# Transposing x with a diagonal of inverse roots at two layer ends of a transformer trunk, instead of scaling it first

## The reference

```python
def rmsnorm(x, g):
    y = xf * lax.rsqrt(jnp.mean(xf * xf, axis=-1, keepdims=True) + EPS)
    return (y * g.astype(jnp.float32)).astype(x.dtype)

def modulate(h, shift, scale):
    return h * (1 + scale[:, None, :]) + shift[:, None, :]

for i in range(DEPTH):
    mod = jnp.einsum('bd,sdk->bsk', cond, ada_w[i]) + ada_b[i]
    ...
    h = modulate(rmsnorm(x, norm_g[i, 0]), shift_t, scale_t)
    y = pool_mixer(...) if i % N_MIXERS == 0 else retention(...)
    x = x + gate_t[:, None, :] * y
    h = modulate(rmsnorm(x, norm_g[i, 1]), shift_m, scale_m)
    x = x + gate_m[:, None, :] * sq_relu_mlp(h, mlp_w1[i], mlp_w2[i])
return rmsnorm(x, final_g)
```

## Time and profile before

| | |
|---|---|
| median of 3 runs | 2337.33 us (2337.26 to 2337.89) |
| the profiled execution's own time | 2337.5 us |
| its span in the profile | 2335.7 us |
| TensorE busy in the span | 2250.4 us, 96% |
| VectorE, ScalarE, GpSimd busy | 72%, 46%, 6% |
| mean granted TensorE clock | 0.987 |

### The profile page before, as it was taken

The page is one execution under the profiler, slowest core; times in us unless marked ns, Lnnn a source line. Parts: engine busy times, 40 slices in busy tenths (PEclk is TensorE's granted clock), DMA queues, the critical chain, the costliest instruction groups (busy, mean ns, idle before and its releaser), DMA issues.

```text
span 2335.7 us, 28480 instructions
## 1 busy us (share of the span) xinstructions
PE 2250.4 (96%) x10021; PEld 1815.4 (78%) x10021; DVE 1679.1 (72%) x1808; ACT 1084.2 (46%) x1340; POOL 139.5 (6%) x249
## 2 busy tenths in 40 slices
PE   5479999999999999999999999999999999999998
PEld 2147788888888887888888888887888888888887
DVE  4678888788887898777676777677877555555556
ACT  2324554544544545444454444555553453453454
POOL 0000000100100100001000001000100000000000
PEclk9699999999999999999999999999999999999999
DMA  9999989998998976878766877876997776776774
GB/s 400 416 413 399 340 294 327 368 363 282 365 333 296 363 274 231 306 263 273 249 226 222 297 258 247 273 235 205 337 357 249 232 231 192 229 229 193 230 229 150
DMA packets 276674, 664.21 MB, mean 284 GB/s; under 512 B 21768, under 2 KB 22200, under 8 KB 269632
## 3 DMA queue, kind: packets, MB, share of 16 engines
q1 hardware_dynamic: 260320, 611.92, 75.4%
q0 software_dynamic: 15328, 49.87, 6.3%
q10 hardware_dynamic: 896, 0.75, 0.1%
HBM read 638.30 MB, written 24.14 MB: 284 GB/s over the span
## 4 chain that ended last, share of the span: by engine, by line
PE 91%; DVE 1%; issue 0%; DMA 0%; ACT 0%; POOLq 0%; POOL 0%; SPq 0%; DVEq 0%; ACTq 0%
PE acc L699 89%; PE acc L1101 1%; PE score_ps L1088 0%; DMA raw<-in_mlp_w 0%; DVE ada_acc L1581 0%; PE score_ps L887 0%; PE tb L827 0%; DVE ev L1877 0%; DVE w_lo L1575 0%; PE tb L962 0%; PE mod_ps L835 0%; DVE x L1881 0%; ACT w_hi L1152 0%; DVE scratch L1747 0%; DVE scratch L1742 0%
## 5 line engine op out<-in xcount | busy, mean ns | idle before, releaser
L1575 DVE TENSOR_TENSOR w_lo<-raw,w_hi 128x1024 fp32r<-128x1024 f32 x775 | 943.3, 1223 | 558.4 <-ACT w_hi L1152 555.7
L1152 ACT ACTIVATE w_hi<-raw 128x1024 fp32r<-128x1024 f32 x775 | 822.0, 1061 | 1094.9 <-PE acc L699 974.9
L699 PE MATMUL acc<-w_hi,h_lo 128*128 128x512 f32 x1788 | 698.7, 391 | 2.0 <-issue 1.6
L699 PE MATMUL acc<-w_hi,h_hi 128*128 128x512 f32 x1788 | 696.2, 389 | 0.0
L699 PE MATMUL acc<-w_lo,h_hi 128*128 128x512 f32 x1788 | 696.0, 389 | 0.0
L699 PE MATMUL acc<-w_hi,a_lo 128*128 128x512 f32 x1312 | 512.0, 390 | 0.4 <-DVE w_lo L1575 0.4
L699 PE MATMUL acc<-w_lo,a_hi 128*128 128x512 f32 x1312 | 511.0, 390 | 0.0
L699 PE MATMUL acc<-w_hi,a_hi 128*128 128x512 f32 x1312 | 510.9, 389 | 0.0
L699 PEld LDWEIGHTS acc<-w_hi,h_lo 128*128 128x128 f32 x1788 | 335.7, 188 | 74.6 <-issue 4.1
L699 PEld LDWEIGHTS acc<-w_hi,h_hi 128*128 128x128 f32 x1788 | 335.6, 188 | 69.8
L699 PEld LDWEIGHTS acc<-w_lo,h_hi 128*128 128x128 f32 x1788 | 335.8, 188 | 68.8
(11 more groups left out here) (201 smaller groups left out, 900.8 us busy)
## 6 DMA issues: line engine op xcount, KB each, us to landing
raw<-in_mlp_w SPq DMA_DIRECT2D x512, 512.0 KB, 5.1
ada_raw<-in_ada_w SPq DMA_DIRECT2D x248, 512.0 KB, 6.7
raw<-in_ret_w_in SPq DMA_DIRECT2D x192, 512.0 KB, 4.5
ada_early_h<-in_ada_w SPq DMA_DIRECT2D x32, 1024.0 KB, 13.3
raw<-in_ret_w_out SPq DMA_DIRECT2D x64, 512.0 KB, 4.4
ada_raw<-in_ada_w SPq DMA_DIRECT2D x16, 1024.0 KB, 12.5
square_blocks<-ev POOLq DMA_DIRECT2D x112, 128.0 KB, 4.9
ev<-square_blocks POOLq DMA_DIRECT2D x28, 512.0 KB, 6.3
```

Source lines behind the costliest of these rows:

```text
L699: mm = nc.tensor.matmul(acc[pair][t][:], l[:, CK * c + j, tok], w[:, slot, j, :], start=first and j == 0 and i == 0, stop=last and j == CK ...
L1152: nc.scalar.activation(w_hi[:, o % RING], raw[:, o % RING], ACT.Copy).then_inc(hi_ready, 1)
L1575: nc.vector.tensor_tensor(w_lo[:, o % RING], raw[:, o % RING], w_hi[:, o % RING].bitcast(F32), ALU.subtract).then_inc(lo_ready, 1)
```

## The change

At the two layer ends, x is no longer scaled into `x_scaled`. VectorE makes one 128x128 diagonal per token tile, the identity times that tile's `rstd`, and `fill(q)` on TensorE multiplies the slices of x itself with it. That product scales and turns in one step. It is an ordinary float32 matmul (`nc.tensor.matmul`), where `nc.tensor.transpose` stood before. In ScalarE's order, tile 0's squares go ahead of `hi(0)`, and `hi(3)` goes behind `fill(0, 1)`. (It is the diff's first `boundary()`; the one with `gated` and `added` is VectorE's.) In VectorE's order, tile 0's mean square and its diagonal go ahead of `lo(0)`, `split_part(0, 0)` goes ahead of `gated(1)`, the eight scalings go, and tile 1's diagonal stands behind `split_part(1, 0)`.

```diff
             def fill(q):
                 t, f = FILLS[q]
-                pe.wait_ge(xs_ready, n.n["XS"] + q + 1)
+                pe.wait_ge(tile_diag, n.n["XS"] // 4 + t + 1)
...
-                    tr = nc.tensor.transpose(fill_ps[f][:, j * P:(j + 1) * P], x_scaled[:, t, k * P:(k + 1) * P],
-                                             ident[:])
+                    tr = nc.tensor.matmul(fill_ps[f][:, j * P:(j + 1) * P], x[:, t, k * P:(k + 1) * P],
+                                          diag[:, t, :], start=True, stop=True)
...
             def boundary():
+                squares(3, True, (0,))
                 hi(0)
-                squares(3, True, (0,))
-                for c in range(1, 4):
-                    hi(c)
+                hi(1)
+                hi(2)
                 act.wait_ge(gain_ready, n.n["GN"] + 1)
                 n.add(GN=1)
                 fill(0, 0)
                 fill(0, 1)
+                hi(3)
                 fill(1, 0)
                 squares(3, True, (1,))
                 fill(1, 1)
...
-            def scale_x(q):
-                t, b = FILLS[q]
+            def diagonal(t):
                 dve.wait_ge(rstd_done, n.n["MS"] + t + 1)
-                blk = slice(b * NB, (b + 1) * NB)
-                nc.vector.tensor_scalar(x_scaled[:, t, blk], x[:, t, blk], rstd[:, t:t + 1], None,
-                                        ALU.mult).then_inc(xs_ready, 1)
+                nc.vector.tensor_scalar(diag[:, t, :], ident[:], rstd[:, t:t + 1], None, ALU.mult).then_inc(tile_diag, 1)
...
             def boundary(gated, added):
                 gated(0)
                 added(0)
+                tile_mean_square(0)
+                diagonal(0)
                 lo(0)
-                tile_mean_square(0)
                 lo(1)
-                scale_x(0)
+                split_part(0, 0)
                 gated(1)
-                scale_x(1)
                 added(1)
-                split_part(0, 0)
-                lo(2)
                 split_part(0, 1)
                 tile_mean_square(1)
+                lo(2)
                 split_part(1, 0)
-                scale_x(2)
-                scale_x(3)
-                scale_x(4)
+                diagonal(1)
                 lo(3)
                 split_part(1, 1)
-                split_part(2, 0)
-                scale_x(5)
-                split_part(2, 1)
-                scale_x(6)
+                split_fill(2)
                 split_fill(3)
                 split_fill(4)
-                scale_x(7)
                 split_fill(5)
```

More of the change, by code:

```diff
@@ L305, in program @@
         y_sum = scratch[:, 2048:6144].rearrange("p (t n) -> p t n", t=TT)
-        x_scaled = y_sum
         mlp_gate = scratch[:, 6144:8192]
@@ L419, in program @@
         tile0_done = sem("tile_0_of_last_unit")
-        xs_ready = sem("x_scaled")
+        tile_diag = sem("diagonal_of_tile")
         norm_T = sem("scaled_x_transposed")
```

## The result

| | before | after |
|---|---|---|
| median of 6 runs each | 2337.89 us (2337.26 to 2339.88) | 2347.17 us (2346.37 to 2348.17) |
| profiled execution, span | 2337.5, 2335.7 us | 2347.33, 2345.5 us |
| mean granted TensorE clock | 0.987 | 0.987 |

The ratio is 1.0039, with a 95% interval of 1.0029 to 1.0049: slower, as forecast. The time lies 2.3 us above the forecast of 2344.9 and 0.7 us above the range.

A forecast was written before the change was run, and what follows sets the result against it. TensorE, busy 96% of the span, was taken as the bound, changeable only at the two layer ends. Each end adds 1.10 + 2.70 = +3.8, both +7.6; 2337.5 + 7.6 = 2345.1, less 0.2 gives 2344.9 us, range 2342.2 to 2346.5.

The forecast's parts named there:

- Fills at 0.90: At the layer ends, a fill of float32 products takes 8 x 0.113 = 0.90 us against 0.44, +0.45 per fill.
- a product costs what a transpose costs: Rival for the fills at the layer ends: +0.65 us at each end, 2338.6 us, no change; chance 0.08.
- First product -0.11, chunk 1 +0.06: First layer end: first new product at 895.18 instead of 895.29, chunk 1 at 897.19 instead of 897.13 us.
- The wait for tile 1's diagonal, 1.04: Ahead of fill 2 at each layer end, TensorE waits 1.04 us for the diagonal, queued behind `lo(2)` and `split_part(1,0)`.
- The diagonal is in time: Rival: tile 1's squares come a microsecond earlier than replayed, without the 1.04 us wait; +5.5, 2342.8 us; chance 0.10.
- 3.8 per end: Each layer end gets 1.10 us up to fill 2 and 2.70 for fills 2 to 7: +3.8.
- the second is its repetition: The second layer end was taken to repeat the first, so one end was worked out and doubled to +7.6 us.
- VectorE time that nobody waited for, except the first one: The eight dropped scalings (0.48 us each, 0.40 apart) gain nothing, except the first, whose place fill 0 takes.
- The clock at 1.00: Granted TensorE clock at the ends stays 1.00; rival: half speed there, +5 us each, 2354.9 (one end 2349.9); chance 0.08.
- I checked that nothing else becomes late: Behind fill 2 at each end, chunks 2 and 3 get their splits and `lo(3)` in time, so nothing is added.
- nothing but these ends: From 886 us on, TensorE's 8 waits, 3.4 us, all lie at the layer ends; nothing else can be shortened.
- The change adds no transfer: GpSimd's and SyncE's queues keep their order and no transfer is added.

The follow-up runs named there:

- products_only: The kernel before with its order and scalings, but float32 products with the identity in place of the fills' transposes; 2345.80 us, ratio 1.0034.
- early_diag: The changed kernel with tile 1's diagonal and `split_part(1, 0)` ahead of `lo(2)`; 2345.36 us, ratio 1.0027 to before.
- gate_first: The changed kernel with tile 1's gate and addition ahead of the first split, its squares behind `fill(0, 0)`; 2343.10 us, ratio 1.0018 to before.
- after_again: The changed kernel once more, in a later session; 2347.28 us, ratio 1.0040 to before.
- after_pad: The changed kernel with 128 more TensorE instructions, waits for a value long reached, at the program's start; 2346.33 us, ratio 1.0035 to before.
- order_only: The kernel before with its transposes and scalings, but the changed kernel's order; 2339.73 us, ratio 1.0003.

## Why the prediction was right, and where it failed

- **Fills at 0.90.** Right: 0.89 from start to start. Seven of them alone are 3.23 (products_only). The 64 records of `norm_fill` were the row that decided it, and "a product costs what a transpose costs" is out.
- **First product -0.11, chunk 1 +0.06.** Right: -0.12 and +0.08 (895.17 and 897.21).
- **The wait for tile 1's diagonal, 1.04.** Right in place and cause, a little too long: fill 2 starts 2.39 behind chunk 1 where 1.47 was due, so 0.92, and 0.82 at the second end. "The diagonal is in time" is out; early_diag, which makes it so, gives 0.8 per end back.
- **3.8 per end.** Right: 3.81 and 3.84. Of what stands behind it, one reading was too simple: "the second is its repetition". There the first product waits for tile 1's gate (`ev`, line 1789): 1.7 us by the list, 0.8 more than at the first end. The second end still costs no more, since the later wait for the diagonal swallows it. That was luck, for the replay doesn't have it. Both waits are gone in gate_first.
- **"VectorE time that nobody waited for, except the first one".** Too simple as well: the four waits for line 1818 in the earlier trace rows are for the first two scalings of each end. The second stood in a gap ahead of the first product that was there anyway, so the sum is not touched.
- **The clock at 1.00.** Right. The half speed of that rival is the 0.50 that the kernel before has from 164 to 170 us, around TensorE's idle 4.4 us ahead of 165.47; no run shows it at a layer end.
- **"I checked that nothing else becomes late", and with it "nothing but these ends".** This is the step that failed: the sum puts everything behind the ends at nothing. The list of waits of before shows none there, and I took this for a property of the stretch, but it held only for where the code lay. The change makes TensorE's program 128 instructions longer, which I had in hand when I counted two records for each product, and the loop at 1980 us then fetches its code again on its second trip. That costs 1.0 us. "The change adds no transfer" failed with it: there are 10 more fetches of code. With the missing term the forecast from the same base is 2337.33 + 7.65 + 1.01 = 2346.0, which is inside the range. The other 1.2 us to the median of after are not settled one by one. Of these, 0.56 is the median of before itself, which three more runs moved from 2337.33 to 2337.89. Waits such as the one at 1117 us, 0.9 in one execution and none in the next, can make up the other 0.6, but that is not shown.

## What to carry to other kernels

On an engine that is 96% busy, an instruction that fuses two steps must be priced by what the busy engine pays: here VectorE was rid of eight scalings at each end, none of which set the pace, and TensorE paid 0.45 us more per fill. This price can be read from the trace if the operation stands anywhere in it. An instruction whose input is not there yet must not stand in a queue ahead of work that is ready; here VectorE waited 1.5 us with tile 1's gate behind it. And where a change adds instructions to an engine that has a loop, look at the lines of code fetches in the two pages (75 and 85 here) and at the place of the jump back, before a microsecond is given to anything else.

## What was not expected of the hardware

- In these nine kernels the jump back of one loop costs TensorE nothing or 0.8 to 1.2 us, and which of the two goes with where the code lies (75 or 76 fetches against 85). Why it is 0.8 in one kernel and 1.2 in another is open.
- GpSimd's inverse root of 128x1 took 1.47 us where 0.56 was forecast, when it started beside a running `lo` on VectorE (897.73 to 898.95), and 0.55 in early_diag, where `lo(2)` comes later:

```profile
897.89 1.47 POOL L2342 TENSOR_TENSOR rstd<-meansq,minus_half 128x1 f32<-128x1 f32 x1 [7.39 <-DVE meansq L1811]
```

```profile
898.08 0.55 POOL L2342 TENSOR_TENSOR rstd<-meansq,minus_half 128x1 f32<-128x1 f32 x1 [7.40 <-DVE meansq L1811]
```

It ended at 899.36, just ahead of the diagonal's turn at 899.52, and cost nothing here. Tile 1's root took 1.46 or 1.47 at both ends of after, after_again, after_pad and order_only, which all have a `lo` start just ahead of it. In the kernel before, tile 0's root takes 0.56 (891.04) although a `lo` starts 0.12 behind it (891.16). What made it longer in the one place and not in the other, no run shows.
